# Two fused transformer blocks: where the second block's modulation rows are multiplied, how the first down product is split, and where GpSimd makes its weight sums

## The reference

```
def conv_ffn(h, w_up, conv_w, conv_b, w_down, rows):
    u = h @ w_up                                  # 1024 -> 5632
    u = conv2d_grid(u, conv_w, rows) + conv_b     # 3x3, depthwise, on an 8 x 64 grid
    gate, val = jnp.split(u, 2, axis=-1)
    return (jax.nn.silu(gate) * val) @ w_down     # 2816 -> 1024

def second_block(...):
    m_lat = jax.nn.silu(c) @ w_mod[l] + b_mod[l]
    m_ctx = jax.nn.silu(c_ctx) @ w_mod[l] + b_mod[l]
    h = modulate_2(rmsnorm(x, norm_mix[l]), sh1, sc1)
    ...
```

## Time and profile before

| | us |
|---|---|
| median of 3 runs | 1893.43 |
| lowest, highest of them | 1893.31, 1903.49 |
| the profiled execution | 1900.21 |
| its span | 1898.6 |

### The profile page before, as it was taken

The page is one execution under the profiler, slowest core; times in us unless marked ns, Lnnn a source line. Parts: engine busy times, 40 slices in busy tenths (PEclk is TensorE's granted clock), DMA queues, the critical chain, the costliest instruction groups (busy, mean ns, idle before and its releaser), DMA issues. The chain is left out here.

```text
span 1898.6 us, 29839 instructions
## 1 busy us (share of the span) xinstructions
PE 1732.2 (91%) x12382; PEld 1156.2 (61%) x12382; DVE 958.8 (50%) x1605; ACT 513.1 (27%) x973; POOL 398.9 (21%) x404
## 2 busy tenths in 40 slices
PE   7999988789999999899999998999979988978887
PEld 3554487778788888788888887744443323323332
DVE  1775885557488888823588888633130010000113
ACT  4223553341355545201211112620031011110101
POOL 0000017600588887400111110100010000000000
PEclk9999999999999999899999999999979989989998
DMA  9453034213432222322584323205389999999994
GB/s 356 177 208 124 17 89 100 56 38 144 155 124 81 86 89 90 114 92 91 187 326 157 116 89 106 78 31 224 131 313 419 426 426 425 426 426 426 425 422 197
DMA packets 80537, 380.03 MB, mean 200 GB/s; under 512 B 34464, under 2 KB 37536, under 8 KB 54672
## 3 DMA queue, kind: packets, MB, share of 16 engines
q1 hardware_dynamic: 70000, 350.03, 47.6%
q0 software_dynamic: 7104, 26.68, 3.8%
q10 hardware_dynamic: 3296, 1.38, 0.3%
HBM read 364.09 MB, written 19.92 MB: 202 GB/s over the span
## 5 line engine op out<-in xcount | busy, mean ns | idle before, releaser
L3947 PE MATMUL psum<-mem 128*64 128x512 f32 x1504 | 361.8, 638 | 23.2 <-DMA mem<-in_w_upe 10.4
L2091 PE MATMUL psum<-mem 128*128 128x256 f32 x1232 | 268.8, 380 | 3.8 <-ACT mem L378 2.7
L3947 PEld LDWEIGHTS psum<-mem 128*64 128x64 f32 x1504 | 116.0, 146 | 249.1 <-issue 242.4
L2091 PEld LDWEIGHTS psum<-mem 128*128 128x128 f32 x1232 | 233.5, 190 | 39.2 <-ACT mem L378 3.2
L3053 PE MATMUL psum<-mem 128*128 128x256 f32 x896 | 196.7, 381 | 3.3 <-DVE mem L3234 2.8
L3053 PEld LDWEIGHTS psum<-mem 128*128 128x128 f32 x896 | 169.9, 190 | 30.0 <-issue 5.3
L2201 DVE SCALAR_TENSOR_TENSOR psum<-mem,psum 128x512 f32<-128x512 f32 x220 | 150.2, 746 | 0.0
L1681 PE MATMUL psum<-mem 128*128 128x256 f32 x616 | 138.1, 384 | 5.2 <-issue 4.6
L1681 PEld LDWEIGHTS psum<-mem 128*128 128x128 f32 x616 | 117.4, 192 | 24.3 <-issue 7.0
L4018 DVE TENSOR_TENSOR mem<-mem,psum 128x512 f32<-128x512 f32 x16 | 11.0, 688 | 234.9 <-issue 202.9
L2048 POOL TENSOR_TENSOR mem<-mem 128x512 f32<-128x512 f32 x88 | 111.6, 1280 | 56.8 <-ACT mem L2071 56.8
(11 more groups left out here) (443 smaller groups left out, 2589.8 us busy)
## 6 DMA issues: line engine op xcount, KB each, us to landing
mem<-in_w_upe SPq DMA_DIRECT2D x30, 2048.0 KB, 25.4
mem<-in_w_gate SPq DMA_DIRECT2D x29, 2048.0 KB, 27.4
mem<-in_w_downe SPq DMA_DIRECT2D x27, 2048.0 KB, 31.7
mem<-in_ada SPq DMA_DIRECT2D x32, 1024.0 KB, 6.8
mem<-in_w_up SPq DMA_DIRECT2D x22, 1024.0 KB, 4.9
mem<-in_ada POOLq DMA_DIRECT2D x16, 1024.0 KB, 7.2
mem<-in_w_in_g SPq DMA_DIRECT2D x12, 1024.0 KB, 5.2
mem<-in_w_down SPq DMA_DIRECT2D x16, 704.0 KB, 4.0
```

Of the source, the lines that this page charges most:

```text
L2091: ins = pe.matmul(bank, w[:, i], rhs[:, i], start=first and i == 0, stop=last and i == self.N - 1, skip_group_check=True)
L3947: last = pe.matmul(bank[halves[h], :], xs[:, kt, halves[h]], pair[h][0][:, kt, cols], start=kt == 0, stop=kt == tiles - 1, skip_group_chec ...
```

## The change

- `MOD_APART` and `load_apart` go. `MOD_LATE` puts slots 3 to 7 into the up loop: TensorE multiplies slot 3 in tile 4, 4 in tile 6, 5 in tile 8, 6 in tile 10 and 7 in tile 12, each ahead of `p7` of that tile. All use bank 7 (`BANKS = (5, 7, 7, 7)`), so ScalarE takes the rows in steps 5, 9 and 13. In the ring each slot's load stands behind the `w_up` tile of its number.
- `down.p2` of pair 0 is split: `do_p2_begun` multiplies the first ten of its eleven pieces (hidden tiles 11 to 20) when `up.made` is 21, `mod.turn` comes behind it, and `do_p2_ended` multiplies the last piece when `up.made` is 22.
- `OWN` becomes a list: tile 20 has four own taps in each row, so ScalarE makes two taps more and GpSimd two joins more for it, and VectorE ten taps and not twelve.
- GpSimd makes `down.s1` and `down.s2` of pair 0 in step 21, between the joins of tile 20 and those of tile 21. `s4` and `s3` stay behind the loop. Before the loop GpSimd now waits for `up.t_made` to be 4.
- The order of the first `w_down` loads is 0, 2, 3, 1; load n + 4 in the ring waits for the user of load n. So load 5 now waits for load 2's user (`p7`), load 6 for that of load 3 (`p4`, `s1`), load 7 for that of load 1 (`p2`, `s4`).
- Places in SBUF are moved so that `s1`, `s2`, `s4`, `t1` and `t2` of the down product lie on dead parts of the up stage; `t2` now lies over the modulation rows, so VectorE waits for `mod.turned` ahead of `make_t2`. `t1` and `t2` have semaphores of their own. VectorE's wait for `up.p3` ahead of `make_t1` is gone.

```diff
-MOD_APART = 6
+MOD_LATE = {4: 3, 6: 4, 8: 5, 10: 6, 12: 7}
...
+    def do_p2_begun(self, pe, p):
+        self.landed(pe, p, 1)
+        for i in range(self.N - 1):
+            pe.matmul(self.bank(self.Z), self.weights(p, 1)[:, i], self.b21[:, i], start=i == 0, stop=False, skip_group_check=True)
+
+    def do_p2_ended(self, pe, p):
+        i = self.N - 1
+        pe.matmul(self.bank(self.Z), self.weights(p, 1)[:, i], self.b21[:, i], start=False, stop=True, skip_group_check=True).then_inc(self.p2, 1)
...
-    OWN = 3
-    OPS = 2 * (9 - OWN)
+    OWN = [3] * (KF - 2) + [4, 3]
...
             for make in (up.make_s1, up.make_s2, up.make_s3, up.make_s4):
                 make(pool, 0)
             up.zero_borders(pool)
+            pool.wait_ge(up.t_made, 4)
             for p in range(KF + 1):
...
                 if p:
-                    up.join(pool, p - 1, 1, 2)
-                    up.join(pool, p - 1, 0, 2)
-            pool.wait_ge(mod.mm, 8)
-            down.make_s1(pool, 0)
-            down.make_s2(pool, 0)
+                    for i in range(2, up.OWN[p - 1]):
+                        up.join(pool, p - 1, 1, i)
+                        up.join(pool, p - 1, 0, i)
+                if p == KF - 1:
+                    pool.wait_ge(up.p5, KF)
+                    down.make_s1(pool, 0)
+                    pool.wait_ge(up.p4, KF)
+                    down.make_s2(pool, 0)
             down.make_s4(pool, 0)
             down.make_s3(pool, 0)
...
+                if m in MOD_LATE:
+                    mod.rows_by_product(pe, MOD_LATE[m])
                 up.do_p7(pe, m)
...
             up.do_p3(pe, KF - 1)
-            for g in range(MOD_EARLY, 8):
-                if g == 4:
-                    pe.wait_ge(up.c21_done, KF)
-                mod.rows_by_product(pe, g)
-            pe.wait_ge(up.made, KF // 2)
             pe.wait_ge(up.c11_done, KF)
             down.do_p1(pe, 0)
+            pe.wait_ge(mod.rows_done, 4)
+            pe.wait_ge(up.made, KF - 1)
+            down.do_p2_begun(pe, 0)
             pe.wait_ge(up.c12_done, KF)
             mod.turn(pe)
-            pe.wait_ge(mod.rows_done, 2)
             pe.wait_ge(up.made, KF)
-            down.do_p2(pe, 0)
+            down.do_p2_ended(pe, 0)
...
                 if 1 <= p <= KF:
-                    up.own_tap(act, p - 1, 0, 2)
+                    for i in range(2, up.OWN[p - 1]):
+                        if i > 2:
+                            up.own_tap(act, p - 1, 1, i)
+                        up.own_tap(act, p - 1, 0, i)
...
             dve.wait_ge(up.made, KF)
-            dve.wait_ge(up.p3, KF)
             down.make_t1(dve)
             down.add_a(dve, 0)
+            dve.wait_ge(mod.turned, 1)
             down.make_t2(dve)
...
-    for g in range(MOD_EARLY, MOD_APART):
-        k.put("ada2", g)
-    for g in range(2 * KD):
+        if m in MOD_LATE:
+            k.put("ada2", MOD_LATE[m])
+    for g in (0, 2, 3, 1, *range(4, 2 * KD)):
         k.put("w_down", g)
```

More of the change, by code:

```diff
@@ L1607, with __init__ @@
     X, Z, W, V = (6, 1), 7, 0, 2
-    def __init__(self, k, before, rhs, gate, x, t_at, t4_at, s_at):
+    def __init__(self, k, before, rhs, gate, x, t1_at, t2_at, t4_at, s_at):
         n, c = self.N, self.COLS
@@ L1614, in __init__ @@
         self.b11, self.b12, self.b21, self.b22 = rhs[:, 0:n, 0:c], rhs[:, 0:n, c:2 * c], rhs[:, n:2 * n, 0:c], rhs[:, n:2 * n, c:2 * c]
-        self.t1, self.t2, self.t3, self.t4 = wide(t_at), wide(t_at + n * c), self.b12, wide(t4_at)
-        self.s1, self.s2, self.s4 = (narrow(s_at + n * P * i) for i in range(3))
+        self.t1, self.t2, self.t3, self.t4 = wide(t1_at), wide(t2_at), self.b12, wide(t4_at)
+        self.s1, self.s2, self.s4 = (narrow(at) for at in s_at)
+        self.t1_made, self.t2_made = k.sem("down_t1"), k.sem("down_t2")
         self.p1, self.p2, self.p3, self.p4, self.p5, self.p6, self.p7 = before.p1, before.p2, before.p3, before.p4, before.p5, before.p6, before.p7
@@ L1665, in make_t1 @@
     def make_t1(self, dve):
-        dve.tensor_tensor(self.t1, self.b12, self.b11, SUB).then_inc(self.t_made, 1)
+        dve.tensor_tensor(self.t1, self.b12, self.b11, SUB).then_inc(self.t1_made, 1)
     def make_t2(self, dve):
-        dve.wait_ge(self.t_made, self.old + 1)
-        dve.tensor_tensor(self.t2, self.b22, self.t1, SUB).then_inc(self.t_made, 1)
+        dve.wait_ge(self.t1_made, 1)
+        dve.tensor_tensor(self.t2, self.b22, self.t1, SUB).then_inc(self.t2_made, 1)
     def make_t3(self, dve):
@@ L1675, in make_t4 @@
     def make_t4(self, dve):
-        dve.wait_ge(self.t_made, self.old + 3)
+        dve.wait_ge(self.t2_made, 1)
         dve.tensor_tensor(self.t4, self.b21, self.t2, SUB).then_inc(self.t_made, 1)
@@ L1702, in do_p4 @@
     def do_p4(self, pe, p):
-        pe.wait_ge(self.t_made, self.old + 4)
+        pe.wait_ge(self.t_made, self.old + 2)
         pe.wait_ge(self.v_added, self.old + p + 1)
@@ L1709, in do_p5 @@
         pe.wait_ge(self.s1_made, self.old + p + 1)
-        pe.wait_ge(self.t_made, self.old + 1)
+        pe.wait_ge(self.t1_made, 1)
         if p:
@@ L1716, in do_p6 @@
         pe.wait_ge(self.s2_made, self.old + p + 1)
-        pe.wait_ge(self.t_made, self.old + 2)
+        pe.wait_ge(self.t2_made, 1)
         pe.wait_ge(self.a_added, self.old + p + 1)
@@ L1722, in do_p7 @@
         pe.wait_ge(self.s3_made, self.old + p + 1)
-        pe.wait_ge(self.t_made, self.old + 3)
+        pe.wait_ge(self.t_made, self.old + 1)
         pe.wait_ge(self.u_added, self.old + p + 1)
@@ L2043, in join, with joins, ops @@
         n = 2 * (i - 1) + 1 - row
-        pool.wait_ge(self.own, 2 * self.OWN * m + self.own_number(row, i))
+        pool.wait_ge(self.own, 2 * sum(self.OWN[:m]) + self.own_number(row, i))
         if i > 1:
-            pool.wait_ge(self.joined, 2 * (self.OWN - 1) * m + n - 1)
+            pool.wait_ge(self.joined, self.joins(m) + n - 1)
         q = self.q[:, m % 2, row]
         pool.tensor_tensor(q, q, self.term[1 - row], ADD).then_inc(self.joined, 1)
+    def joins(self, m):
+        return 2 * sum(n - 1 for n in self.OWN[:m])
+    def ops(self, m):
+        return 2 * (9 - self.OWN[m])
     def own_number(self, row, i):
@@ L2054, in own_tap @@
     def own_tap(self, act, m, row, i):
-        before = self.joined, 2 * (self.OWN - 1) * m + 2 * (i - 2) + 2 - row
+        before = self.joined, self.joins(m) + 2 * (i - 2) + 2 - row
         if i == 0:
@@ L2188, in taps @@
         for j in range(first, end):
-            i, row = self.OWN + j // 2, j % 2
+            i, row = self.OWN[m] + j // 2, j % 2
             a = self.acc(row).rearrange("p (r c) -> p r c", r=ROWS)
@@ L2195, in taps @@
                     dve.wait_ge(self.c21_done, m + 1)
-                dve.wait_ge(self.joined, 2 * (self.OWN - 1) * m + 2 * (self.OWN - 1) - row)
+                dve.wait_ge(self.joined, self.joins(m + 1) - row)
                 base = self.q[:, m % 2, row]
             else:
-                dve.wait_ge(self.tap, (self.OPS - 2) * m + j - 1)
+                dve.wait_ge(self.tap, sum(self.ops(x) - 2 for x in range(m)) + j - 1)
                 base = a
@@ L2210, with __init__ @@
 class SecondMod:
[L2212 to L2216, removed]
+    BANKS, TURNED = (5, 7, 7, 7), 4
+    def __init__(self, k, rows, c32):
+        self.k, self.rows, self.c32 = k, rows, c32
         self.mm, self.rows_done, self.turned, self.added, self.ready = (k.sem("mod2_" + n) for n in ("mm", "rows", "turned", "added", "c32"))
-        for g in range(MOD_APART):
+        for g in range(8):
             k.freed[k.number("ada2", g)] = [(self.mm, g + 1)]
-    def load_apart(self, sp):
-        for w, g in zip(self.apart, range(MOD_APART, 8)):
-            sp.dma_start(w, self.k.d["ada2"][g]).then_inc(self.apart_landed, 16)
     def rows_by_product(self, pe, g):
         k = self.k
[L2227 to L2234, removed]
+        n = k.number("ada2", g)
+        k.weights_ready(pe, n)
+        w = k.slot(n).rearrange("p (k m) -> p k m", k=KD)
         if g == 0:
             pe.wait_ge(self.ready, 1)
+        if g in (4, 6):
+            pe.wait_ge(self.rows_done, g // 2)
         for kt in range(KD):
@@ L2633, in _ @@
         def _(sp):
[L2634 to L2636 removed]
+            k.send_weights(sp, k.number("w_down", 1) + 1)
             sp.wait_ge(up.p3, KF)
@@ L2770, in _ @@
                     up.c21(act, p)
-                if p == KF + 1:
-                    for b in range(1, 4):
-                        mod.take_rows(act, b)
+                if p in (5, 9, 13):
+                    mod.take_rows(act, (p - 1) // 4)
             warm_root(k, act)
@@ L2915, in block_one @@
     norm2, gains2 = Norm(k, "norm2", 22528, k.bank[4], k.bank[6]), k.small[:, 16:24]
-    mod = SecondMod(k, k.at(25600, 2048), k.at(25088, 256).rearrange("p (k m) -> p k m", k=KD), [k.at(17408 + SLOT * i, SLOT) for i in range(2)])
+    mod = SecondMod(k, k.at(25600, 2048), k.at(25088, 256).rearrange("p (k m) -> p k m", k=KD))
```

6 lines of the change are left out of this document (3 added, 3 removed).

## The result

The changed kernel's median is 1911.19 us over six runs (1906.26 to 1913.40), the kernel before 1896.34 over six (1893.31 to 1903.49). The ratio is 1.007 with an interval of 1.0053 to 1.0086: 13 us slower, 10 to 16. It is a small loss in per cent and well clear of the noise. The profiled execution's span is 1911.0 us against 1898.6, +12.4.

What follows compares the result with a forecast made beforehand. TensorE bounds the up loop, VectorE's last 24 taps the tail. Slots +4.46, late joins +3.1, split -4.33, clock and turn order the rest: +3.3 us, median 1893.4 to 1896.7, range 1889.5 to 1904.

Steps and rivals of the forecast that it cites:

- the likeliest case: Whole kernel, rival A: 3.3 us slower, median 1896.7 us, chance 0.6.
- slots in the loop: Up loop: five slots lengthen it by 0.89 us each, so everything waiting for the last gate comes 4.46 us later.
- own taps of tile 20: VectorE's tile 20: two taps fewer save 1.34 us, waiting for extra joins costs 0.7, net gain 0.6 us.
- sums ahead of tile 21's joins: GpSimd's last tile: s1 and s2 delay the joins, so tile 21's first tap starts at 773.7, not 769.9 old time.
- taps that wait for GpSimd's sums: VectorE beside GpSimd's moved sums: sharing SBUF interfaces changes no term of the sum.
- The rest of pair 0: Down product behind the turn: 68 instructions take 14.7 us at full clock, VectorE's sums stay hidden, p7 starts 3.3 us later.
- rival D: GpSimd's sums stretch 1 us beside VectorE's taps, with a full second clock fall and late loads: +6.7 us, chance 0.15.
- the idle TensorE behind `p1`: TensorE ahead of the begun part of p2: idle over 7 us, waiting for tile 20's gate.
- The begun part: Split p2 of pair 0: twenty instructions take 5.8 to 6.8 us, starting at half clock.
- The down loads: Pair 1's loads 6 and 7 land together, later by nothing to 1.7 us; hidden, +0.7 us if both errors add.
- C: Up loop: the slots vanish in it, S near 0, giving -1.2 us, 1892.2 us; chance 0.05.
- B: GpSimd's last tile: its two sums are hidden, p7 starts at 798.7, -3.2 us, 1890.2 us; chance 0.2.

Runs made afterwards that it cites:

- e9_slots_wait: Kernel before with slots 3 to 7 inside the up loop, and GpSimd's s1 held until VectorE's first two taps of tile 21; ratio to before 1.0031.
- e6_own: As e5_turns, with four own taps a row in tile 20 and their joins, as in the change; ratio to before 0.9983.
- e5_turns: Kernel before with p2 split, GpSimd's s1, s2, s4 held until VectorE's first two taps of tile 21, s3 moved to VectorE; ratio to before 0.9992.
- e1_wait: Changed kernel with two GpSimd waits: s1, s2 behind VectorE's first two taps of tile 20, s4, s3 behind those of tile 21; ratio to before 1.0031.
- e7_behind: Changed kernel with all four GpSimd sums of pair 0 behind tile 21's joins and VectorE's first two taps of it; ratio to before 1.0027.
- e2_cut: Changed kernel with each of GpSimd's four sums of pair 0 cut into four shorter instructions, no wait added; ratio to before 1.0053.
- e8_psum: Changed kernel with one input of each row's first tap in tiles 20 and 21 in PSUM, their bias and own taps left out; ratio to before 1.0025.
- e4_split: Kernel before with only the second product of pair 0 split around the turn; ratio to before 0.9986.

## Why the prediction was wrong

**The measured loss of 13 us lies outside the range.** The chances by the 1% bound held; the likeliest case, +3.3 us, had the right sign and a quarter of the size. The last gate was forecast 7.6 us late and was 17.5 us late. The runs divide that:

| part | forecast | measured | from |
|---|---|---|---|
| slots in the loop | +4.46 | +6.0 | e9_slots_wait against before |
| own taps of tile 20 | -0.6 | +1.1 | e6_own against e5_turns |
| sums ahead of tile 21's joins | +3.7 | +3.5 | e1_wait against e7_behind |
| taps that wait for GpSimd's sums | 0 | +6.9 | after against e1_wait |

The parts add up to the 17.5, but the last two depend on the order of counting. The four stalled taps stood for 11.4 us in all (7.13 + 7.14 - 2 x 1.42), and 4.5 of these lie over the wait for the late joins, which was 4.70 us in e1_wait and 0.17 in the changed kernel.

**The step that failed** is in "The rest of pair 0". I read `t1` at 5.16 and `s3` at 6.03 as two instructions that stretch each other, priced it as hidden, and wrote of the sentence from the Trainium skill beside it that it changes no term of the sum. So the taps that would stand for the sums entered the sum at nothing, and they cost 6.9 us at the last gate. The rows said more. `t1` ends at 784.54, and `s3` ends at 787.57, 3.03 later, about what such a sum takes alone (3.17): `s3` had not been slowed, it had not begun. The same rule then had to be asked of every two-input instruction of VectorE that the moved sums would now lie beside, and the first taps of tiles 20 and 21 are such. In rival D I gave it 1 us, from a join of 1.76 beside a tap. But there the join came second and waited for a tap: it was issued at 762.17 and the taps ended at 762.80, so 0.63 of its 1.76 us are wait. The price of a collision is the rest of the other engine's instruction. A tap is 0.7 us long, `s1` and `s2` are 3.2.

The Trainium skill (GPSIMD Engine Reference, section 1) says that GpSimd's SBUF interfaces are shared with VectorE's instructions that have two SBUF inputs. The runs agree as to which instructions: 3.6 us with two SBUF inputs, 0.7 with one in PSUM. In that section the Trainium skill speaks of contention and gives no size.

**The slots** were right in kind and too cheap: "TensorE neither wins nor loses" fell with the 0.3 us a slot for going in and out of the loop, 1.5 in all. That the tail behind the loop is paid in full was right (e9_slots_wait: 6.0 at the gate, 6.5 at `p7`).

**The own taps** were wrong in sign. The two late arrivals were small as forecast, but the chain from `c12` through ScalarE and GpSimd back to tile 21's first tap was not followed, and a collision with a join lay in it.

**The late joins** were priced right where nothing else is in the way (3.7 forecast, 3.5 between e7_behind and e1_wait, with the SiLU of tile 20 queued behind them). In the changed kernel itself GpSimd's list was not what held them. I had forecast GpSimd without a gap up to the last join, and it sat idle for 2.11 us ahead of the last three, waiting for ScalarE's own taps. These waited for `c12` of tile 21 (778.00), which stood on VectorE behind the stalled taps of tile 20.

**Right** were the idle TensorE behind `p1` and the distance from the last gate to `p7` (18.2 forecast, 18.0 measured, 22.6 before). That last agrees by other parts than mine. The gate came so late that the turn was hidden, and the clock fell in the wait behind it. TensorE by short stretches in the kernel after (length, busy, granted clock, DMA share, GB/s):

```profile
774.00:783.30 9.30, 0.00 (x0) 0.59 0.02 9
783.33:788.00 4.67, 4.67 (x11) 0.50 0.00 0
788.00:790.60 2.60, 2.60 (x10) 0.75 0.00 0
790.70:794.30 3.60, 3.60 (x33) 1.00 0.56 200
794.40:798.30 3.90, 0.00 (x0) 0.72 0.00 0
798.40:803.00 4.60, 4.60 (x11) 0.50 0.00 0
```

The begun part took 7.51 us, above the 5.8 to 6.8 that I had worked out from the two recoveries of the trace before (the longer one ended nearer to 784.56 than to 784.45, by the mean of 0.61 in the earlier trace rows, which changes nothing): here the half clock (1.2 GHz) lasted to about 789.3, 6.0 us of work. In e1_wait the 66 instructions behind a turn without a wait took 14.45 us, all at full clock (2.4 GHz), so a turn alone didn't bring the clock down there.

**The down loads** went as forecast: VectorE's `s1` of pair 1 waited 5.41 us for its load and not 3.61, and `p6` of the pair was no later. GpSimd's wait for `t_made` cost nothing: the loop took 262.8 us from the mark to the start of its last product in the changed kernel and in e9_slots_wait, which lacks that wait.

**The rivals.** C, that the slots vanish in the loop, is refuted by the 25.42 us and by the 6.0 at the gate. B lacked the time that GpSimd needs, as said against it. D named the mechanism with 1 us where it cost 6.9.

## What to carry to other kernels

Before moving work onto GpSimd, list VectorE's instructions with two SBUF inputs that it will lie beside; each that falls into a long GpSimd instruction waited here for the rest of it, so long sums belong where VectorE reads PSUM or is idle, or have to be cut into short ones. When an instruction's time in a trace is double its usual, look whether the two ends lie one usual length apart: then it waited, and its price elsewhere is set by its neighbour's length. Work taken out of a gap beside a critical tail and put into a saturated loop lengthens everything behind the loop by its full time plus the change over, however idle the other engines are.

## What the runs showed of the hardware that I had not expected

A VectorE `scalar_tensor_tensor` with two SBUF inputs and a GpSimd `tensor_tensor` in SBUF don't overlap here: a tap took 3.58 to 3.65 us beside sums of 3.16 to 3.60 us (after), 1.41 to 1.49 beside sums of 0.9 (e2_cut), and 0.76 alone (before). It works both ways: GpSimd's `s3` took 6.01 to 6.03 us when it was issued while VectorE's `t1` was at work (before, e7_behind, e9_slots_wait) and 3.17 to 3.18 alone (e4_split, e1_wait). In these rows the one that was issued second waited. With one of the two inputs in PSUM the same VectorE instruction took 0.75 us beside a GpSimd sum of 3.18 (e8_psum). That a GpSimd instruction which only writes, or one with a single input, would do the same is not shown.
